# Two of the first six units of row work moved ahead of the second block's queries, on TensorE and ScalarE

## The reference

```python
h = h + mixer_block(rmsnorm(h, g_mix), ...)          # MLA attention and a short convolution
h = h + memory_xattn(rmsnorm(h, g_x), ...)           # 4 heads over 256 memory tokens
h = h + peer_ffn(rmsnorm(h, g_ffn), ...)             # product-key experts
out = rmsnorm(h, g_final)

# peer_ffn, per token t and head (8 heads, top 16 of 128 x 128 experts):
q = xt @ w_pq                                        # queries, two halves of 64 per head
s = q . sub_keys                                     # scores of both halves against 128 keys
experts, best = top-16 pairs of the two top-16 lists
gates = softmax(best)
a = gelu(xt . u_experts[experts]) * gates
out_t = sum over heads and 16 experts: a * v_experts[expert]
```

## Time and profile before

| | us |
|---|---|
| median of 3 runs | 3288.43 (3287.04 to 3289.13) |
| profiled execution | 3278.33, span 3276.5 |
| busy PE / DVE | 2589.3 / 2290.5 |
| busy ACT / POOL | 1352.8 / 1228.2 |
| DMA | 1242.16 MB, mean 379 GB/s |

### The profile page before, as it was taken

The page is one execution under the profiler, slowest core; times in us unless marked ns, Lnnn a source line. Parts: engine busy times, 40 slices in busy tenths (PEclk is TensorE's granted clock), DMA queues, the critical chain, the costliest instruction groups (busy, mean ns, idle before and its releaser), DMA issues.

```text
span 3276.5 us, 28771 instructions
## 1 busy us (share of the span) xinstructions
PE 2589.3 (79%) x7912; PEld 1400.7 (43%) x7912; DVE 2290.5 (70%) x4808; ACT 1352.8 (41%) x3634; POOL 1228.2 (37%) x1051
## 2 busy tenths in 40 slices
PE   8988889778878888787877888887878666666675
PEld 7764556344335554443344554553334222222222
DVE  2031577887776877888776877878786877687765
ACT  1122343484434334754433344764433333333333
POOL 0000143344344443344344433333445444444443
PEclk9989999988988999899998999899989888898888
DMA  7442499999999999999999999999999999999998
GB/s 269 157 184 103 175 394 418 411 370 398 421 421 398 412 419 408 394 414 420 420 410 421 417 420 397 351 403 411 418 408 422 421 421 418 421 412 413 415 421 338
DMA packets 186034, 1242.16 MB, mean 379 GB/s; under 512 B 21905, under 2 KB 31121, under 8 KB 39953
## 3 DMA queue, kind: packets, MB, share of 16 engines
q0 software_dynamic: 147456, 1073.81, 80.0%
q1 hardware_dynamic: 36112, 153.93, 12.1%
q10 hardware_dynamic: 2304, 12.58, 0.9%
HBM read 1223.73 MB, written 16.52 MB: 379 GB/s over the span
## 4 chain that ended last, share of the span: by engine, by line
DMA 38%; PE 28%; DVE 17%; ACT 6%; issue 5%; POOL 3%; DVEq 3%; ACTq 0%; SPq 0%; POOLq 0%
DMA rows<-in_experts,idx 38%; PE ps L1031 10%; PE ps L1064 5%; DVE rows L1493 5%; PE ps L1050 5%; DVE acc_v L1504 4%; POOL rows L682 3%; PE ps L1089 2%; ACT L842 1%; PE ps L1102 1%; PE ps L1107 1%; DVE gsq L1660 1%; ACT probs L842 1%; PE ps L1194 1%; PE ps L1223 1%
## 5 line engine op out<-in xcount | busy, mean ns | idle before, releaser
L682 POOL DMA_INDIRECT rows<-in_experts,idx x1024 | 1224.4, 1196 | 2023.8 <-PE ps L1031 846.5
L1031 PE MATMUL ps<-rows,diag 128*128 128x512 f32 x2712 | 1435.2, 667 | 502.8 <-ACT diag L735 458.7
L1493 DVE CUSTOM_DVE_ANT_0 rows<-rows,hn 128x1024 f32<-128x1024 f32 x1024 | 1238.0, 1224 | 573.5 <-DMA rows<-in_experts,idx 552.3
L1031 PEld LDWEIGHTS ps<-rows,diag 128*128 128x128 f32 x2712 | 539.4, 210 | 1235.7 <-ACT diag L735 707.6
L724 ACT ACTIVATE gelu<-dots 128x1 f32<-128x1 f32 x1024 | 206.8, 202 | 1418.6 <-DVE dots L1493 1402.0
L1504 DVE SCALAR_TENSOR_TENSOR acc_v<-rows,weight,acc_v 128x1024 f32<-128x1024 f32 x346 | 443.7, 1282 | 0.6 <-ACT weight L728 0.6
L1064 PE MATMUL ps<-T,wbuf 128*128 128x256 f32 x1536 | 365.2, 390 | 18.0 <-ACT T L886 8.7
L1064 PEld LDWEIGHTS ps<-T,wbuf 128*128 128x128 f32 x1536 | 299.4, 196 | 109.2 <-issue 51.0
L728 ACT ACTIVATE weight<-gelu,gate 128x1 f32<-128x1 f32 x1024 | 301.7, 295 | 74.6 <-issue 3.1
L1050 PE MATMUL ps<-wbuf,T 128*128 128x512 f32 x640 | 307.5, 619 | 22.6 <-ACT T L886 20.0
L735 ACT ACTIVATE diag<-ident,weight 128x128 f32<-128x128 f32 x678 | 272.3, 402 | 56.1 <-issue 1.1
(11 more groups left out here) (205 smaller groups left out, 1906.9 us busy)
## 6 DMA issues: line engine op xcount, KB each, us to landing
wbuf<-in_w_conv SPq DMA_DIRECT2D x24, 1024.0 KB, 10.1
wbuf<-in_w_o SPq DMA_DIRECT2D x16, 1024.0 KB, 9.9
wbuf<-in_w_pq SPq DMA_DIRECT2D x16, 1024.0 KB, 10.2
rows<-in_experts,idx POOLq DMA_INDIRECT x1024, 13.1
wbuf<-cross_a SPq DMA_DIRECT2D x12, 1024.0 KB, 13.7
wbuf<-cross_b SPq DMA_DIRECT2D x12, 1024.0 KB, 13.6
wbuf<-in_w_xkv SPq DMA_DIRECT2D x7, 1024.0 KB, 9.5
wbuf<-in_w_cq SPq DMA_DIRECT2D x8, 768.0 KB, 9.0
```

The costliest lines, as they stand in the source:

```text
L682: pool.indirect_dma_start(out=rows[n % RR][:], out_offset=None, in_=w["experts"][:, :], in_offset=bass.IndirectOffsetOnAxis(ap=idx[:, b % ...
L1031: mm = pe.matmul(ps[:, 6 + half, :], diag[:, m % DIAGS, :], rows[n % RR][:, D + half * HALFC:D + (half + 1) * HALFC], start=(k == 0), stop ...
L1493: dve.tensor_tensor_reduce(out=rows[n % RR][:, 0:D], in0=rows[n % RR][:, 0:D], in1=hn[:, b % 3, :], scale=1.0, scalar=0.0, op0=ALU.mult, o ...
```

## The change

The six units of group 0 are taken in another order on PE and ACT. Two are taken after the turns of the second block's normed stream and ahead of `block_queries(1)` (PE) and `block_queries_out(1)` (ACT). The other four are spread two by two over `queries(2)` and `queries(3)`, where there were three and three. DVE takes six as before. Group 1 and later are the same.

```diff
 FIRST_UNITS = 6
-ROOMS = [dict((stage, FIRST_UNITS // 2 if stage == "pq" else 0) for stage in ROOM)] + ...
+EARLY_UNITS = 2
+ROOMS = [dict((stage, (FIRST_UNITS - EARLY_UNITS) // 2 if stage == "pq" else 0) for stage in ROOM)] + ...
...
# ACT, front of group 0
                     for i in range(2, 4):
                         turned_out("nT", i, T)
+                    take(work, EARLY_UNITS)
                     block_queries_out(1)
                     scores_out(1, 0)
...
# PE, front of group 0
                     for i in range(2, 4):
                         turn_normed(i)
+                    take(work, EARLY_UNITS)
                     block_queries(1)
                     scores(1, 0)
...
# DVE, front of group 0
-                    take(work, 2 * ROOMS[g]["pq"])
+                    take(work, EARLY_UNITS + 2 * ROOMS[g]["pq"])
```

More of the change, by code:

```diff
@@ L79 @@
 FIRST_UNITS = 6
-ROOMS = [dict((stage, FIRST_UNITS // 2 if stage == "pq" else 0) for stage in ROOM)] + [dict((stage, n - (FEWER.get(stage, 0) if g == 1 else 0)) for stage, n in ROOM.items()) for g in range(1, NG)]
+EARLY_UNITS = 2
+ROOMS = [dict((stage, (FIRST_UNITS - EARLY_UNITS) // 2 if stage == "pq" else 0) for stage in ROOM)] + [dict((stage, n - (FEWER.get(stage, 0) if g == 1 else 0)) for stage, n in ROOM.items()) for g in range(1, NG)]
 STAGES = [("x", 1), ("xT", 2 * HB), ("c", 3), ("kr", 1), ("gc", 2), ("hx", 2), ("gb", 2), ("q", 2 * HB), ("kv", 2 * HB),
```

## The result

| | before | changed |
|---|---|---|
| median (8 runs each) | 3288.78 us (3283.63 to 3290.41) | 3298.71 us (3295.09 to 3302.25) |
| profiled execution | 3278.33, span 3276.5 | 3296.84, span 3295.0 |

The changed kernel is slower: ratio 1.0035, 95% interval 1.0023 to 1.0048, that is 11.5 us (7.6 to 15.8), or 9.9 us between the medians. In a later set of runs the same kernel gave 1.0029 (1.0019 to 1.0040), medians 9.7 us apart. The forecast was 3298.3.

The account below looks back on a forecast made before the run. TensorE was taken to bound 370 to 420 us: first diagonal at 385.6, rows 5.8, queries 7.4, remainder 29.0 put ACT's last score copies at 427.8, 10.1 us later. Carrying 9.9 gave 3298.3 us, range 3290 to 3302.5.

Parts of the forecast that it names:

- No cost on DVE, ACT's exp hidden in its idle time: DVE's order costs nothing; ACT's 3.7 us first part fits its idle 10.30 us, removing DVE's 6.59 us wait.
- TensorE idles until the first diagonal: Ahead of the second block's queries TensorE waits for row 0's diagonal until 385.6: 10.65 us lost.
- Rows 0 and 1 at the lower clock: After idling, TensorE's first two row matmuls run slowly: 5.8 us, bounds 4.5 to 6.9.
- Queries at full clock behind them: The second block's queries follow the two rows on TensorE at full clock: 7.4 us, ending at 398.8.
- From there to the meeting point: From the second block's queries' end to ACT's last score copies, which everything later awaits: 29.0 us, reaching 427.8.
- The chunk's wait: TensorE's 1.04 us wait for a w_pq weight chunk, issued when the second block's queries end, moves along; bounds 0 and 2.
- All of it carried to the end: ACT's last score copies come 10.1 us later and the end shifts with them, 9.9 us after small savings; chance 0.74.
- swallowed: Rival: the late front is made up while expert rows stream; profiled 3286 to 3293 us, no change; chance 0.13.
- DVE's stall: Rival: DVE's 6.59 us wait for ACT's exp was the bound, so removing it gives 3281.8 us profiled; chance 0.05.
- passing: Rival: TensorE runs the second block's queries while a row's diagonal is missing; about 0 to -3 us; chance 0.02.
- clock down through the queries: Rival: TensorE's clock stays low, the second block's queries take 10.2 us instead of 7.4; +12.7, 3301.1 us; chance 0.06.
- offset of 10.1 us between profiled execution and median: Whole kernel: the median was taken to stand 10.1 us above the profiled execution, turning 3288.2 into 3298.3 us.

Follow-up runs that it names:

- experiment 3: Kernel before with ACT's copy of h and exp of the first gates moved ahead of its copy of the second block's queries; ratio 0.9992 against before.
- Experiment 6: Changed kernel with 10, then 12 unused matmuls filling TensorE's wait for the first diagonal; ratios 1.0015 and 1.0020 against before.
- experiment 5: Kernel before with 12 unused matmuls on TensorE between the second block's first scores and the next queries; ratio 1.0028 against before.
- Experiment 7: Kernel before with 5 unused matmuls in TensorE's idle time ahead of the second block's turns; ratio 0.9989 against before.
- experiment 4: Changed kernel with four units ahead of the second block's queries instead of two; ratio 1.0049 against before.
- experiment 1: Changed kernel with TensorE's two early units put back behind the second block's queries, ACT as changed; ratio 0.9998 against before.
- experiment 8: Kernel before with ACT's exp early and two units moved behind the second block's first scores, 0.9994; last run also fills TensorE's idle times, 0.9990.

## Why the prediction was right

- *No cost on DVE, ACT's exp hidden in its idle time*: right. ACT ready at T + 6.4 (forecast T + 6.3), DVE's stall gone (one reading in it was off: ACT's idle 10.30 us, which end at 385.19, lie mostly ahead of DVE's wait of 384.07 to 390.66 and not in the same time), and worth nothing that can be measured (experiment 3).
- *TensorE idles until the first diagonal*: rows start at T + 13.25, forecast T + 13.3. The idle 11.28 us was said as "some 11".
- *Rows 0 and 1 at the lower clock*: the mis-sized term. 5.8 us forecast, 6.5 from their start to that of the queries (6.62 with the last record's end), within the bound of 6.9; the clock came back only when both rows were nearly done. Experiment 6 shows that it is the clock (3.60 with it up).
- *Queries at full clock behind them*: 7.3 us, forecast 7.4. Ends at T + 27.05, forecast T + 26.5.
- *From there to the meeting point*: 28.7 us, forecast 29.0. The chunk's wait moved along, 1.12 us. Row 10 was issued at 416.35 and landed in 5.6 us, not in the 9.4 of the forecast, so its dot came at 423.2; ACT's sixth unit was over at 427.2, TensorE's last queries at 431.4, so the spare was 4 us, not 2.
- *All of it carried to the end*: shown by the times, 7.6 to 15.8 us against 10.4 to 11.6 of stretch, and by experiment 5. That the rest is 2858.9 against 2858.8 is partly luck, since it varies by 12 us between traces.

Step by step from one trace to the other: start of rows instead of queries +10.60, rows +6.46, queries -2.90, tail -3.76: +10.40; forecast +10.1. Against the second trace of before it is 11.6, mainly since there the queries took 8.79 us. So the mechanism was right, but that the medians moved by 9.9 us, just as forecast, is luck: the stretch gives 10.4 to 11.6, and the interval is 8 us wide. Of the rivals, "swallowed", "DVE's stall" and "passing" are out by experiments 5, 3 and the idle 11.28 us itself; "clock down through the queries" did not happen.

One thing the forecast had wrong in its account, without effect on the number: the offset of 10.1 us between profiled execution and median was treated as fixed. The profiled execution of the changed kernel took 3296.84, not 3288.2, 1.9 under its median. Eight of the 10.1 were that one early front ahead of T.

And one thing it weighed wrongly: it credited the queries' return to full clock in full against before. Experiment 7 has the slow queries of the old order partly hidden behind the chunk, which landed at T + 17.8 there and in the first trace of before alike. In the changed order the chunk is issued after the queries in any case, so against the first trace of before the account came out the same.

## What to carry to other kernels

An engine that has no reason to wait must not get an instruction with a late input ahead of ready work: on an in-order queue it costs the time until the input comes, in which the ready work could have run. The price is paid once, however few instructions wait; a longer list can add to it in other ways (4.3 us in experiment 4). Before moving work forward, write down when its input is first ready and what stands ready behind it; here 384.07 for the first dot and 374.95 for the queries settled the case. Where everything meets at one point and nothing behind it is tied to absolute time, the delay at that point is the delay at the end.

## What the runs showed of the hardware

- A 1 MB chunk took between 4.8 and 8.5 us to land: 4.89 us with two gathers issued 10 and 7 us ahead, 6.60 with six, 8.5 with the ring of eight still landing (389.25 to 397.76). A load issued 3.6 us earlier in that crowd landed no earlier (experiment 7). The gathers under way are not all of it: with the same eight at the same distances it took 5.4 us in one trace and 8.0 in another (experiment 3), and why stays open.
- The clock sometimes fell after short waits. After 1.99 us idle, following 9.5 us of matmuls without a gap, the granted clock was 0.50 for the next 2 us. But after 1.84 us idle (experiment 1) and 2.40 us (the last run of experiment 8, two rows from 433.64 in 3.70 us) it stayed at 1.00, so the length of the wait alone doesn't tell. After 4.69 us idle it was still 0.50 when 4 us of work had been done. A wait for the chunk costs about half its length again in slow matmuls: 12 records took 5.49 instead of 2.86 us behind 4.69 us, 4.54 behind 4.20, and 24 took 1.6 us more behind 2.82.
- T, ahead of which all programs are the same but for the unused matmuls of two of them, ran from 372.30 to 382.58, and the rest of the changed kernel differed by 10 us, while the stretch repeats within 0.1 us for the changed kernel and within 1.3 for before. The granted clock over 200 to 265 us was 0.76 in the early trace and 0.67 in the second of before.
